# Two cross attentions of a two-block transformer on one core: the four heads laid between the query and output projections

## The reference, cut to what matters

```python
def mem_cross_attention(h, mem, norm_mem, w_q, w_kv, w_o):
    m = rms_norm(mem, norm_mem)
    q = (h @ w_q).reshape(B, S, MEM_HEADS, MEM_HEAD_DIM)       # 4 heads of 256
    k, v = jnp.split(m @ w_kv, 2, axis=-1)
    ...
    s = jnp.einsum('bqhd,bkhd->bhqk', q, k).astype(jnp.float32) * (MEM_HEAD_DIM ** -0.5)
    p = jax.nn.softmax(s, axis=-1).astype(v.dtype)
    o = jnp.einsum('bhqk,bkhd->bqhd', p, v).reshape(B, S, D_MODEL)
    return o @ w_o

x = x + mem_cross_attention(rms_norm(x, xa_norm_x[layer]), mem, ...)
x = x + swiglu(rms_norm(x, ffn_norm[layer]), ffn_w_gate_up[layer], ffn_w_down[layer])
```

## Time and profile before

| | us |
|---|---|
| median of 3 runs | 1770.91 (1770.7 to 1777.75) |
| the profiled execution, its own time | 1766.2 |
| its span | 1764.4 |
| PE busy | 1661.0 (94%) |
| DVE busy | 1287.3 (73%) |
| ACT busy | 1024.3 (58%) |
| mean granted clock of PE | 0.981 |

### The profile page before, as it was taken

One profiled execution on the slowest core, in us unless ns is written; L12 is line 12 of the kernel. 1 busy time (PEld: TensorE's weight loads), 2 busy tenths in 40 slices (PEclk: granted clock), 3 DMA queues, 4 the chain that ended last, 5 costly groups with the idle time before them and its releaser, 6 DMA issues.

```text
span 1764.4 us, 29591 instructions
## 1 busy us (share of the span) xinstructions
PE 1661.0 (94%) x11478; PEld 1486.4 (84%) x11478; DVE 1287.3 (73%) x1439; ACT 1024.3 (58%) x1127; POOL 63.9 (4%) x56
## 2 busy tenths in 40 slices
PE   8999989799999999999989879899999999799998
PEld 7998879788877776777769768899998999799997
DVE  6546887755789999999977867675556888575554
ACT  4333674455689999999975454353434484353342
POOL 0000000000000000000015400000000020000000
PEclk9999999899999999999999989999999999999999
DMA  9662123265799999999995423355554555255540
GB/s 327 191 186 90 61 78 118 104 262 214 275 397 422 422 422 423 423 423 422 422 344 201 143 96 120 120 176 182 190 174 136 166 193 173 72 186 173 185 143 25
DMA packets 186768, 391.74 MB, mean 222 GB/s; under 512 B 6960, under 2 KB 152112, under 8 KB 162096
## 3 DMA queue, kind: packets, MB, share of 16 engines
q1 hardware_dynamic: 185008, 383.89, 59.3%
q0 software_dynamic: 1664, 6.52, 1.0%
HBM read 379.77 MB, written 10.62 MB: 221 GB/s over the span
## 4 chain that ended last, share of the span: by engine, by line
PE 63%; DVE 15%; DMA 12%; issue 6%; ACT 4%; DVEq 0%; SPq 0%; POOL 0%; ACTq 0%; POOLq 0%
DMA raw<-w_e_up_dram 10%; PE ps L672 10%; PE ps L673 10%; PE ps L677 10%; DVE wlo L1996 7%; PE ps L1081 5%; PE ps L1036 3%; PE ps L1030 3%; PE ps L967 2%; PE ps L969 2%; PE ps L975 2%; PE ps L1032 2%; ACT whi L1408 1%; PE ps L760 1%; PE ps L762 1%
## 5 line engine op out<-in xcount | busy, mean ns | idle before, releaser
L1996 DVE TENSOR_TENSOR wlo<-raw,whi 128x2048 fp32r<-128x2048 f32 (+3 forms) x358 | 812.6, 2281 | 223.1 <-ACT whi L1408 216.2
L1408 ACT ACTIVATE whi<-raw 128x2048 fp32r<-128x2048 f32 (+3 forms) x358 | 675.6, 1890 | 338.0 <-PE ps L677 196.3
L672 PE MATMUL ps<-xh,whi 128*128 128x256 f32 x800 | 200.6, 290 | 11.7 <-DVE xl L2009 10.6
L673 PE MATMUL ps<-xl,whi 128*128 128x256 f32 x800 | 197.9, 286 | 0.0
L672 PE MATMUL ps<-xb_h,whi 128*128 128x256 f32 x768 | 186.9, 284 | 5.2 <-DVE arena L2078 5.2
L673 PE MATMUL ps<-xb_l,whi 128*128 128x256 f32 x768 | 186.3, 283 | 0.0
L672 PEld LDWEIGHTS ps<-xh,whi 128*128 128x128 f32 x800 | 156.1, 195 | 13.4 <-issue 11.5
L1030 PE MATMUL ps<-whi,xh 128*128 128x512 f32 x528 | 160.4, 396 | 0.1
L673 PEld LDWEIGHTS ps<-xl,whi 128*128 128x128 f32 x800 | 156.2, 195 | 0.2
L672 PEld LDWEIGHTS ps<-xb_h,whi 128*128 128x128 f32 x768 | 147.4, 192 | 5.7 <-DVE arena L2078 5.6
L673 PEld LDWEIGHTS ps<-xb_l,whi 128*128 128x128 f32 x768 | 147.4, 192 | 0.1
(11 more groups left out here) (432 smaller groups left out, 2845.4 us busy)
## 6 DMA issues: line engine op xcount, KB each, us to landing
raw<-w_e_gate_dram SPq DMA_DIRECT2D x64, 1024.0 KB, 10.7
raw<-w_e_up_dram SPq DMA_DIRECT2D x64, 1024.0 KB, 10.5
raw<-w_e_down_dram SPq DMA_DIRECT2D x64, 1024.0 KB, 10.5
raw<-ffn_w_gate_up_dram SPq DMA_DIRECT2D x44, 1024.0 KB, 5.0
raw<-w_in_dram SPq DMA_DIRECT2D x30, 1024.0 KB, 5.5
raw<-ffn_w_down_dram SPq DMA_DIRECT2D x22, 1024.0 KB, 4.9
raw<-xa_w_kv_dram SPq DMA_DIRECT2D x16, 1024.0 KB, 5.6
raw<-xa_w_q_dram SPq DMA_DIRECT2D x8, 1024.0 KB, 5.3
```

Source lines behind the costliest of these rows:

```text
L672: nc.tensor.matmul(o[b], wh, h, start=b == 0 and a == 0, stop=False, skip_group_check=True)
L673: nc.tensor.matmul(o[b], wh, l, start=False, stop=False, skip_group_check=True)
L1408: nc.scalar.activation(whi[u % HL][:, 0:n], raw[u % RAW][:, 0:n], ACT.Copy).then_inc(hi_ready, 1)
L1996: v.tensor_tensor(wlo[u % HL][:, 0:n], raw[u % RAW][:, 0:n], whi[u % HL][:, 0:n].bitcast(F32), ALU.subtract).then_inc(lo_ready, 1)
```

## The change

All three `cross(l)` functions are written anew, and nothing outside them changes but the PSUM banks of this attention.

- Scores of a head's first 128 queries go to bank 0, those of the other 128 to bank 1. PE issues both in one go (`scores`), then both halves' transposes (`turns`, banks 2 and 3), then both halves' products with the values (`mixes`, bank 4 or 5).
- The calls of `all_out` give way to `out_of`, a wait for one unit.
- The order on PE is q0, q1, scores 0, q2, turns 0, scores 1, q3, mixes 0, turns 1, scores 2, then the first two output units in four pieces (`both_some`, each with 2 of the 8 input chunks for both units, that is 24 matmuls), with mixes 1, turns 2, scores 3 behind the first piece, mixes 2, turns 3, mixes 3 behind the second.
- The copies to `xq` (line 2203), `split_highs` and `split_lows` go. ACT makes the high part of a head's output straight from PSUM (`out_high`), DVE the low part (`out_low`), two chunks a head.
- o2 and o3 follow as before. The squares of o0 are summed behind the fourth piece, those of o1 behind o2, those of o2 behind o3.

The diff:

```diff
@@ -398,6 +398,8 @@
                     bank, at = 1, step["head"] * T
             else:
                 bank, at = g, step["qt"] * T if step["kind"] == "swa" else 0
+                if step["kind"] == "xa":
+                    bank = step["qt"]
             return ps[:, bank, at:at + step["nk"]]
 
         def gather_bank(c, low):
@@ -1346,19 +1348,95 @@
 
             def cross(l):
 
-                opening(lin_bank(), u_xa[l][0][0], xb_h, xb_l)
-                feature_unit(u_xa[l][0][1], xb_h, xb_l)
-                all_out()
-
-                def queries_between(a):
-                    if a in (2, 4):
-                        all_out()
-                    if a in (0, 2):
-                        feature_unit(u_xa[l][0][2 + a // 2], xb_h, xb_l)
-
-                attend(steps_x[l], PT_later, queries_between)
-                st["fresh"] = True
-                residual(u_xa[l][1], bank=3)
+                uq, uo = u_xa[l]
+                base, first = st["step"], st["lin"]
+
+                def out_of(m):
+                    pe.wait_ge(lin_evac[m % 2], m // 2 + 1)
+
+                def scores(h):
+
+                    if h >= 1:
+                        pe.wait_ge(att_biased, base + 2 * h)
+                    for step in steps_x[l][2 * h:2 * h + 2]:
+                        for a, (q, k) in enumerate(step["scores"][0]):
+                            mm = nc.tensor.matmul(score_bank(step, 0), q, k, start=a == 0, stop=a == 1)
+                    mm.then_inc(att_scored, 2)
+
+                def turns(h):
+
+                    pe.wait_ge(att_pt, base + 2 * h)
+                    for qt in range(2):
+                        s = base + 2 * h + qt
+                        pe.wait_ge(att_probs, s + 1)
+                        for kt in range(2):
+                            mm = nc.tensor.transpose(ps[:, 2 + qt, kt * P:kt * P + P],
+                                                     S[s % 3][:, 0, kt * P:kt * P + P], ident)
+                        mm.then_inc(att_turned, 1)
+
+                def mixes(h):
+
+                    pe.wait_ge(att_pt, base + 2 * h + 2)
+                    if h == 0:
+                        pe.wait_ge(att_out, st["y"])
+                    for qt, step in enumerate(steps_x[l][2 * h:2 * h + 2]):
+                        for _, k, pv in step["pv"]:
+                            at = k * T + qt * P
+                            for a, (v, g, kt) in enumerate(pv):
+                                mm = nc.tensor.matmul(ps[:, 4 + h % 2, at:at + P], v, PT_later[qt][:, kt, :],
+                                                      start=a == 0, stop=a == 1)
+                    mm.then_inc(att_mixed, 2)
+
+                def both_some(o, ks):
+
+                    for n, u in enumerate(uo[0:2]):
+                        if ks[0] == 0:
+                            weights_in(u)
+                        if n == 0:
+                            split_in()
+                        wh, wl = wview(whi, u, DC, 256), wview(wlo, u, DC, 256)
+                        for b in range(2):
+                            for k in ks:
+                                cols = slice(b * P, b * P + P)
+                                nc.tensor.matmul(o[n][:, b, :], wh[:, k, cols], xh[:, k, :], start=b == 0 and k == 0,
+                                                 stop=False, skip_group_check=True)
+                                nc.tensor.matmul(o[n][:, b, :], wh[:, k, cols], xl[:, k, :], start=False, stop=False,
+                                                 skip_group_check=True)
+                                mm = nc.tensor.matmul(o[n][:, b, :], wl[:, k, cols], xh[:, k, :], start=False,
+                                                      stop=b == 1 and k == 7, skip_group_check=True)
+                        if ks[-1] == 7:
+                            mm.then_inc(unit_used, 1)
+
+                opening(lin_bank(), uq[0], xb_h, xb_l)
+                feature_unit(uq[1], xb_h, xb_l)
+                out_of(first)
+                scores(0)
+                feature_unit(uq[2], xb_h, xb_l)
+                turns(0)
+                out_of(first + 1)
+                scores(1)
+                feature_unit(uq[3], xb_h, xb_l)
+                mixes(0)
+                turns(1)
+                out_of(first + 2)
+                scores(2)
+                o = [lin_bank(), lin_bank()]
+                both_some(o, (0, 1))
+                mixes(1)
+                turns(2)
+                out_of(first + 3)
+                scores(3)
+                both_some(o, (2, 3))
+                mixes(2)
+                turns(3)
+                mixes(3)
+                both_some(o, (4, 5))
+                both_some(o, (6, 7))
+                st["step"] += 2 * XA_H
+                for a in range(3):
+                    if a:
+                        feature_unit(uo[a + 1])
+                    squares(2 * a, DC, bank=3)
 
             cross(0)
             gated(ffn[0][0], ffn[0][1], trio0[0])
@@ -1517,8 +1595,9 @@
                 if s >= 2:
                     act.wait_ge(att_mixed, s - 1)
                 n = len(step["scores"]) * step["nk"] // P
+                bank = 2 + step["qt"] if step["kind"] == "xa" else 2
                 last = nc.scalar.activation(PT[s % 2][:, 0:min(n, 4), :],
-                                            ps[:, 2, 0:min(n, 4) * P].rearrange("p (b q) -> p b q", q=P), ACT.Copy)
+                                            ps[:, bank, 0:min(n, 4) * P].rearrange("p (b q) -> p b q", q=P), ACT.Copy)
                 if n > 4:
                     last = nc.scalar.activation(PT[s % 2][:, 4:n, :],
                                                 ps[:, 3, 0:(n - 4) * P].rearrange("p (b q) -> p b q", q=P), ACT.Copy)
@@ -1898,18 +1977,44 @@
 
             def cross(l):
 
-                uq = u_xa[l][0]
+                uq, uo = u_xa[l]
+                base = st["step"]
+
+                def exps_of(h):
+                    for a in (2 * h, 2 * h + 1):
+                        exps(base + a, steps_x[l][a])
+
+                def copies_of(h):
+                    for a in (2 * h, 2 * h + 1):
+                        copy_turned(base + a, steps_x[l][a], PT_later)
+
+                def out_high(h):
+
+                    act.wait_ge(att_mixed, base + 2 * h + 2)
+                    nc.scalar.activation(xh[:, 2 * h:2 * h + 2, :], ps[:, 4 + h % 2, :].rearrange("p (c t) -> p c t", c=2),
+                                         ACT.Copy).then_inc(xh_ready, 1)
+                    st["split"] += 1
+
                 ahead(uq[0])
                 root()
-                stage(uq[0:2])
-
-                def queries_out(a):
-                    if a in (0, 2):
-                        ahead(uq[2 + a // 2])
-                        st["lin"] += 1
-
-                attend(steps_x[l], PT_later, queries_out)
-                split_highs(xq, uq[-1] + 1)
+                ahead(uq[1])
+                exps_of(0)
+                ahead(uq[2])
+                copies_of(0)
+                ahead(uq[3])
+                exps_of(1)
+                ahead(uo[0])
+                out_high(0)
+                copies_of(1)
+                exps_of(2)
+                out_high(1)
+                copies_of(2)
+                exps_of(3)
+                copies_of(3)
+                out_high(2)
+                out_high(3)
+                st["step"] += 2 * XA_H
+                st["lin"] += XA_H
                 residual(u_xa[l][1], f"ffn{l}", xb_h)
                 ahead(ffn[l][0])
                 root()
@@ -2782,18 +2887,50 @@
 
             def cross(l):
 
-                rooted(u_xa[l][0][0])
-                stage(u_xa[l][0][0:2], lambda a: xq[:, 2 * a:2 * a + 2, :])
-
-                def queries_ahead(a):
-                    if a in (1, 3):
-                        h = 2 + a // 2
-                        ahead(u_xa[l][0][h])
-                        scaled_out(u_xa[l][0][h], xq[:, 2 * h:2 * h + 2, :])
-
-                attend(steps_x[l], lambda k, w: xq[:, k:k + w, :], queries_ahead)
-                dve.sem_inc(h_ready, 4)
-                split_lows(xq, u_xa[l][0][-1] + 1)
+                uq, uo = u_xa[l]
+                base = st["step"]
+
+                def biased_of(h):
+                    for a in (2 * h, 2 * h + 1):
+                        bias_max(base + a, steps_x[l][a])
+
+                def probs_of(h):
+                    for a in (2 * h, 2 * h + 1):
+                        probs(base + a, steps_x[l][a])
+
+                def query_out(h):
+                    scaled_out(uq[h], xq[:, 2 * h:2 * h + 2, :])
+
+                def out_low(h):
+
+                    st["split"] += 1
+                    dve.wait_ge(xh_ready, st["split"])
+                    two = slice(2 * h, 2 * h + 2)
+                    v.tensor_tensor(xl[:, two, :], ps[:, 4 + h % 2, :].rearrange("p (c t) -> p c t", c=2),
```

(24 more changed lines are left out.)

## The result

| | before | after |
|---|---|---|
| median, us | 1773.43 (1770.70 to 1777.75, 4 runs) | 1742.08 (1741.79 to 1742.18, 4 runs) |
| the profiled execution, us | 1766.2 | 1742.06 |
| mean granted clock of PE | 0.981 | 0.981 |

The ratio of after to before is 0.9829 (95% interval 0.9810 to 0.9849): 31 us faster, where 23 were forecast. The profiled executions differ by 24.1 us. The time was forecast at 1748, in a range of 1740 to 1758.

What follows compares the result with a forecast made beforehand. It took hand-over waits in the cross attentions, with no engine the bound there, as the loss: 14.6 + 11.6 - 2 x 1.3 = 23.6, taken as 23 us, off the 1770.9 median gives 1748, 8-in-10 range 1740 to 1758.

Steps and rivals of the forecast that it cites:

- The lay-out of the stage: End of q1 to end of o1 in each cross attention: 39.6 us for 54.24 and 51.24, 14.6 and 11.6 less.
- The split from PSUM: Head outputs split straight from PSUM: 0.6 us on ACT, 0.69 on DVE, no dearer; a 0.69 us copy a head goes.
- the tight place: Head 1's low part ahead of the second piece: ready 0.3 us before its need, at most 0.4 us a head there.
- The tail: End of o1 to end of feed-forward opening: some 20.2 us, some 1.3 us lost in each cross attention.
- DVE's 2 us in the feed-forward part: DVE enters the feed-forward part 2 us late, covered by its earlier 3.13 us idle, which falls to about 1.
- DMAs and POOL: Weight loads and the memory reload after the first cross attention: cost 0, ends 0 and 1 us for loads.
- The sum: Whole kernel: 23.6 us less, 23 after restarts; 1743 us for an execution like the profiled one.
- from the profile to the median: Whole kernel: the same 23 us taken from the median of 1770.9, 4.7 above the profiled execution, giving 1748 us.
- more is gained: Restarts cost less and clock dips near the stage go, the loop's 4 us at most; 1741 to 1744 us, chance 0.08.
- Less is gained: Tight places in the cross attentions missed, DVE's lateness carried on: 8 to 12 us lost, 1756 to 1760, chance 0.14.
- Slower by the clock: PE at the lower clock for half of each stage: 40 us more, less the 23, gives 1788; chance 0.03.
- No change: New waits in the cross attentions serialise as the old ones did; 1765 to 1772 us, chance 0.04.

Runs made afterwards that it cites:

- e3: The changed kernel, but DVE copies each head's output from PSUM to SBUF and both parts are made from that copy; median 1745.00 us.
- e6: The changed kernel, but in the third and fourth pieces the first output unit's 24 matmuls come before the second's; median 1740.99 us.
- e5: The kernel before, with matmuls nobody reads put on PE in four gaps of each cross attention; median 1764.67 us, ratio 0.9972.
- e10: The kernel before, unchanged, profiled once more; 1768.49 us.
- e11: The kernel before, unchanged, profiled once more as a further sample; 1770.91 us.
- e8: The changed kernel as it stands, measured again on the same chip as other experiments; median 1743.91 us.
- e9: The changed kernel with mixes 2 earlier, half pieces on each side of turns 3, and the first output unit ended earlier; median 1742.58 us.
- e12: The changed kernel as it stands, profiled once more; 1743.08 us.
- e4: The kernel before in its old order, with only PE's waits for both linear banks narrowed to one unit; median 1761.55 us, ratio 0.9942.
- e2: The changed kernel, but the first two output units run whole behind the last head, with no pieces between heads; median 1750.59 us.

## Why the prediction was right, and where it was not

**The lay-out of the stage: right.** 39.6 us predicted, 39.53 measured in both. The 0.7 us ahead of mixes 3 are 0.53 idle and a restart. `out_low` 1 was to end 0.3 us ahead of its need; it ends at 1113.33 and the second piece starts at 1113.55, 0.2 us. e3 shows that this is where a later DVE is felt first. Two steps' scores stream in 1.55 us, not 1.72, 0.7 us less over four heads, which the restarts took back. PE is busy 39.00 of 39.53 us, 98.7%.

**The split from PSUM: right.** 0.6 and 0.69 us predicted, 0.595 and 0.690 measured. What the missing copies are worth was left within the lay-out, with the tight place as the only one that feels it; e3 puts them at 1.1 us a cross attention, 0.8 at that place and 0.3 at the first piece, where the lay-out had 0.5 us of cover.

**The tail: right in form.** From the end of o1 to the end of the opening 20.2 us predicted, 1147.20 - 1127.09 = 20.11 measured, for 18.96 before. The wait for the squares is 0.53 for 0.7. At the end of the opening it is 1147.20 - 1145.06 = 2.14 us behind the last squares for 1.86 before, so 0.3 us are lost for 0.5. e6 shows the first to be a wait for o0 and nothing else.

**DVE's 2 us in the feed-forward part: right.** DVE's timeline of after, o0 taken out, o1 taken out, and the row that answers to the last of the earlier trace rows:
```profile
1125.92 0.69 DVE L2231 TENSOR_TENSOR x<-ps,x 128x512 f32<-128x512 f32 x1 [2.99 <-PE ps L1405]
...
1131.60 0.68 DVE L2231 TENSOR_TENSOR x<-ps,x 128x512 f32<-128x512 f32 x1
...
1153.16 0.69 DVE L2525 TENSOR_TENSOR scr<-ps,rstd 128x512 f32<-128x512 f32 x1 [0.98 <-PE ps L679]
```
The round is 5.68 us (5.76 assumed), and the idle of 3.13 us is 0.98: DVE caught up 2.2 us out of it, and PE's loop did not grow. The rest of the execution is 1611.8 us for 1611.0, within the 3.6 by which it moves in any kernel; DMAs and POOL cost nothing to be seen.

**The sum: right for the profiled execution.** 23 us predicted, 24.1 measured; 1743 for such an execution, 1742.06 measured.

**The step that failed: from the profile to the median.** The prediction took 3.0 us of slow clock from the first cross attention as a part of what goes (2.6 by e5), and then set the same 23 us against the median, 4.7 us above the profile, as if these 4.7 were something that both kernels share. They are not. The profile of before held 2.6 us of falls in its cross attentions, e10's 2.6 and e11's 5.7, 3.6 on average, and e11 comes to 1770.9, the median of the first three runs. That the 4.7 us of those runs were falls too is likely and not shown, since they were not profiled. The new order has none of these gaps, and its profile and its median agree (1742.06 and 1742.08, 1744.35 and 1743.91 in e8). The right sum was 21.8 us for the order and, as an estimate from three executions, 3.6 for falls: 25.4 us. The medians differ by 25.2 (before and e8, on one chip) and 31.3 (the first comparison, in which two of before's four runs are its slow ones, 1776 and 1778). The time, 1742.08, lies in the range of the rival "more is gained" (1741 to 1744), and not in the 1744 to 1754 of the forecast; the range of 8 in 10, 1740 to 1758, still holds it. That rival's reason, dips of the clock that go, was the right one at the wrong place: it had them in the loop behind, where the clock is 0.98 as before, and they are in the cross attentions of the old order (e10, e11).

**Left open.** Before's slowest runs, 1776 to 1778 us, lie 5 us above e11, and no profile of one was taken. The clock of the whole run says that they lose more by it: of the 28 runs of before beside the experiments, all nine from 1772.0 us up have a mean clock of 0.973 to 0.976, and the 19 below have 0.977 to 0.981; the new order's runs (after, e3, e6 to e9, e12) have 0.978 to 0.983. Where in the execution they lose it is not shown; falls behind the gaps of 2.3 to 2.7 us too, as in e4 and e11, are the nearest candidate. Nor is it known what moves the part ahead of the first cross attention by 4 us; e5 and after e8 spread by 4.6 and 2.9 us with no fall in the cross attentions of their profiles.

**The rivals.** "Less is gained" needed more than 2 us a cross attention of waits for `xl` among the pieces; there is none. "Slower by the clock" needed 0.3 of the stages at the lower level; it was 1.00 throughout. The Trainium skill ("TensorE: Matmul & The Clock Gate", section "A second HAM failure mode: psum-queue depth-cycling") tells of a clock that swings when short idles interrupt a cycle through banks. The new order goes round six banks and shows no swing with 0.53 us as its longest idle; e2, with the same banks and single idles of 0.9 to 1.5 us between groups, shows a fall in one of its two cross attentions. "No change" falls with 39.53 us.

## What to carry to other kernels

Where PE waits though no engine is a bound, lay the consumer's inputs one unit of independent work ahead: most of the gain here came from the place of the scores and of the pieces, nearly two fifths from narrower waits (e4). An idle of 3 us costs its own length and, six times of nine here, 1.5 to 2.6 us of slow clock, so price a gap with its fall. Look for falls behind every gap before a length is compared: e4's whole stretch showed half of what its waits had brought. And ask how many falls the median holds before a profile's offset is carried over to a kernel that has no such gap. Before a value is copied out of PSUM for two engines to read, compare their durations on the two sources: at 128x512 in f32 they were the same.

## What had not been expected of the hardware

- The clock's fall at a gap of 2.9 to 3.1 us differs from one execution of the same program to the next, 6 of 9. Where it began in the gap it cost 2.6 to 2.7 us: the two stretches of 3 us behind it run at 0.50 and 0.68 (e11), and the next one at 1.00. Where it began later it cost about 1.5.
- It fell behind shorter gaps too: three times of 16 behind single gaps of 2.3 to 2.7 us (e4 twice, e11), and once behind 1.50, 0.26 and 0.47 us within 2 us (e2).
- Filling such a gap with matmuls that nobody reads makes the kernel faster (e5, 4.4 us): 112 matmuls more, 1764.67 for 1769.1.
- A step's scores cost 0.78 us in a pair (1.55 for two), less than the 0.86 of one with a turn behind it. Why was not tested.
